# A first attention block whose turned probabilities and outputs are taken out of PSUM by ScalarE, one and two steps behind its exponentials

## The reference, cut to what matters

```python
s = jnp.einsum('bqhgd,bkhd->bhgqk', q_blk, k_blk).astype(jnp.float32) * scale
s = jnp.where(valid, s, MASK_VALUE)
m = jnp.maximum(jnp.max(s, axis=-1, keepdims=True), sink)
p = jnp.exp(s - m)
p = p / (jnp.sum(p, axis=-1, keepdims=True) + jnp.exp(sink - m))
return jnp.einsum('bhgqk,bkhd->bqhgd', p.astype(v_blk.dtype), v_blk)
```

```python
z = y @ w_glu.astype(jnp.float32) + b_glu.astype(jnp.float32)
out = z[..., :SSM_WIDTH] * jax.nn.sigmoid(z[..., SSM_WIDTH:])
```

## Time and profile before

| what | value |
|---|---|
| runs of the kernel, us | 2356.20, 2364.24, 8599.52 |
| median, us | 2364.24 |
| profiled execution, us | 2353.87, of which the span from first to last instruction 2352.0 |
| TensorE matmuls busy | 2193.4 us, 93% of the span |
| VectorE busy | 1278.7 us, 54% |
| ScalarE busy | 901.6 us, 38% |
| GpSimd busy | 91.5 us, 4% |
| granted TensorE clock, mean | 0.961 |
| first turn's eight steps | about 159.5 to 202 us |
| second turn's eight steps | about 207.2 to 251 us |

### The profile page before, as it was taken

The page is one execution under the profiler, slowest core; times in us unless marked ns, Lnnn a source line. Parts: engine busy times, 40 slices in busy tenths (PEclk is TensorE's granted clock), DMA queues, the critical chain, the costliest instruction groups (busy, mean ns, idle before and its releaser), DMA issues.

```text
span 2352.0 us, 29837 instructions
## 1 busy us (share of the span) xinstructions
PE 2193.4 (93%) x11134; PEld 1795.0 (76%) x11134; DVE 1278.7 (54%) x1993; ACT 901.6 (38%) x1299; POOL 91.5 (4%) x99
## 2 busy tenths in 40 slices
PE   7858899999998999999997899999999978999997
PEld 6735778888876888888875788888777867888886
DVE  6965454434445566655565743244568876433444
ACT  4224332322225556555642432232244424422422
POOL 1000120000040000000000000000000000000000
PEclk9979899999999999999998999999899989999998
DMA  4001213232132222222211222232112212232221
GB/s 160 29 10 37 89 54 107 77 105 105 69 110 81 81 85 69 80 72 85 76 67 39 76 101 90 91 105 90 63 63 72 71 55 72 89 99 98 89 90 54
DMA packets 32091, 185.54 MB, mean 79 GB/s; under 512 B 4736, under 2 KB 5120, under 8 KB 13312
## 3 DMA queue, kind: packets, MB, share of 16 engines
q1 hardware_dynamic: 27216, 176.17, 21.7%
q10 hardware_dynamic: 2736, 6.00, 0.7%
q0 software_dynamic: 2048, 2.17, 0.4%
HBM read 180.06 MB, written 2.10 MB: 77 GB/s over the span
## 4 chain that ended last, share of the span: by engine, by line
PE 82%; DVE 10%; DVEq 4%; ACT 2%; issue 2%; ACTq 0%; DMA 0%; POOL 0%; POOLq 0%
PE ps L517 12%; PE ps L518 12%; PE ps L519 12%; PE ps L908 5%; PE ps L910 5%; PE ps L909 5%; PE ps L950 3%; PE ps L951 3%; PE ps L952 3%; PE ps L540 2%; PE ps L579 2%; PE ps L542 2%; PE ps L541 2%; DVE f_run L2245 1%; PE ps L846 1%
## 5 line engine op out<-in xcount | busy, mean ns | idle before, releaser
L1084 ACT ACTIVATE w_hi<-raw 128x2048 fp32r<-128x2048 f32 x122 | 232.8, 1908 | 298.0 <-PE ps L519 217.0
L517 PE MATMUL ps<-x_hi,w_lo 128*128 128x512 f32 x864 | 336.9, 390 | 5.8 <-DVE w_lo L1481 3.6
L519 PE MATMUL ps<-x_hi,w_hi 128*128 128x512 f32 x864 | 336.2, 389 | 0.0
L518 PE MATMUL ps<-x_lo,w_hi 128*128 128x512 f32 x864 | 336.2, 389 | 0.0
L1481 DVE TENSOR_TENSOR w_lo<-raw,w_hi 128x2048 fp32r<-128x2048 f32 x122 | 280.0, 2295 | 83.3 <-ACT w_hi L1084 82.9
L908 PE MATMUL ps<-x_hi,w_lo 128*128 128x512 f32 x560 | 225.2, 402 | 6.3 <-DVE w_lo L2061 6.3
L910 PE MATMUL ps<-x_hi,w_hi 128*128 128x512 f32 x560 | 219.6, 392 | 0.0
L909 PE MATMUL ps<-x_lo,w_hi 128*128 128x512 f32 x560 | 218.5, 390 | 0.0
L517 PEld LDWEIGHTS ps<-x_hi,w_lo 128*128 128x128 f32 x864 | 162.2, 188 | 41.5 <-DVE w_lo L1481 4.5
L519 PEld LDWEIGHTS ps<-x_hi,w_hi 128*128 128x128 f32 x864 | 162.2, 188 | 33.8
L518 PEld LDWEIGHTS ps<-x_lo,w_hi 128*128 128x128 f32 x864 | 162.2, 188 | 33.2
(11 more groups left out here) (403 smaller groups left out, 4020.0 us busy)
## 6 DMA issues: line engine op xcount, KB each, us to landing
raw<-w_attn_in SPq DMA_DIRECT2D x32, 1024.0 KB, 4.9
raw<-w_gate_up SPq DMA_DIRECT2D x22, 1024.0 KB, 4.9
raw<-w_up_a SPq DMA_DIRECT2D x16, 1024.0 KB, 4.9
raw<-w_down_a SPq DMA_DIRECT2D x16, 1024.0 KB, 4.9
raw<-w_up_h SPq DMA_DIRECT2D x16, 1024.0 KB, 4.9
raw<-w_down_h SPq DMA_DIRECT2D x16, 1024.0 KB, 4.8
raw<-w_hgrn_in SPq DMA_DIRECT2D x8, 1024.0 KB, 4.9
raw<-w_down SPq DMA_DIRECT2D x8, 768.0 KB, 4.3
```

Of the source, the lines that this page charges most:

```text
L517: pe.matmul(o, w_lo[:, slot, a:a + P], hi[:, k, :], start=k == 0, stop=False)
L518: pe.matmul(o, w_hi[:, slot, a:a + P], lo[:, k, :], start=False, stop=False)
L519: last = pe.matmul(o, w_hi[:, slot, a:a + P], hi[:, k, :], start=False, stop=k == st.kc - 1)
L1084: act.activation(w_hi[:, slot, :], raw[:, slot, :], ACT.Copy).then_inc(whi_ready, 1)
```

## The change

The copy of the turned probabilities and the two scalings of the outputs go from VectorE to ScalarE. On ScalarE, step s now holds the exponentials of s, then `turned_out(s-1)` (the copy), then `scale_out(s-2)` (the scalings, written as a Copy with a per-row scale). Behind step 7 stand `turned_out(7)`, `scale_out(6)` and `scale_out(7)`, and then `gate(1, i)`. `gate(0, i)` stands behind `scale_out(3)`. VectorE keeps the sum and the reciprocal (`invert1`), which now wait for `p1_ready` and tell ScalarE by a new semaphore, `inv1_ready`. TensorE's list doesn't change.

```diff
--- before.py
+++ after.py
@@ -357,6 +357,7 @@
     p1t_done, p1t_ready = sem("p1t_done"), sem("p1t_ready")
     o1_done, o1_ready = sem("o1_done"), sem("o1_ready")
     o1t_done = sem("o1t_done")
+    inv1_ready = sem("inv1_ready")
     h_back = sem("h_back")
     vt2_done = sem("vt2_done")
     rot_ready = sem("rot_ready")
@@ -1172,6 +1173,20 @@
                 act.activation(tmp[:, c, :], ps[:, GLU_BANKS[2 * c + 1], :], ACT.Sigmoid,
                                bias=gains[:, ds(2 * i + GAIN_AT["b_glu"] + 4 + c, 1)]).then_inc(gate_ready, 1)
 
+            def turned_out(s, i):
+                n = BLOCKS1[s % 4][1]
+                act.wait_ge(p1t_done, 8 * i + s + 1)
+                act.activation(p1_t[:, s % 2, 0:2 * n * P], ps[:, (5, SUM)[s % 2], 0:2 * n * P], ACT.Copy).then_inc(p1t_ready, 1)
+
+            def scale_out(s, i):
+                hh, b = s // 4, BLOCKS1[s % 4][0]
+                act.wait_ge(o1_done, 8 * i + s + 1)
+                act.wait_ge(inv1_ready, 8 * i + s + 1)
+                for m in range(2):
+                    last = act.activation(o1_tok[:, b, ds(256 * i + 128 * m + 64 * hh, 64)], ps[:, 6, 64 * m:64 * m + 64],
+                                          ACT.Copy, scale=stat[:, s % 4, 12 + m:13 + m])
+                last.then_inc(o1_ready, 1)
+
             with act.Fori(0, 2) as i:
                 for s in range(8):
                     hh, (b, n) = s // 4, BLOCKS1[s % 4]
@@ -1185,8 +1200,15 @@
                         act.activation(p1[:, s % 4, 2 * P * m:2 * P * m + n * P], ps[:, 3 + s % 2, 2 * P * m:2 * P * m + n * P],
                                        ACT.Exp, bias=st_[:, 4 + m:5 + m], scale=0.125, accum_out=st_[:, 8 + m:9 + m])
                     act.activation(st_[:, 6:8], st_[:, 6:8], ACT.Exp).then_inc(p1_ready, 1)
+                    if s >= 1:
+                        turned_out(s - 1, i)
+                    if s >= 2:
+                        scale_out(s - 2, i)
                     if s == 5:
                         gate(0, i)
+                turned_out(7, i)
+                scale_out(6, i)
+                scale_out(7, i)
                 gate(1, i)
 
 
@@ -1844,35 +1866,23 @@
                     ts(st_[:, 4:6], st_[:, 2:4], -1.0, None, ALU.mult)
                     tt(st_[:, 6:8], sinks, st_[:, 2:4], ALU.subtract).then_inc(max1_ready, 1)
 
-                def scale1(s):
-                    hh, (b, n) = s // 4, BLOCKS1[s % 4]
+                def invert1(s):
                     st_ = stat[:, s % 4, :]
+                    dve.wait_ge(p1_ready, 8 * i + s + 1)
                     tt(st_[:, 10:12], st_[:, 6:8], st_[:, 8:10], ALU.add)
                     settle()
-                    dve.reciprocal(st_[:, 12:14], st_[:, 10:12])
-                    settle()
-                    dve.wait_ge(o1_done, 8 * i + s + 1)
-                    for m in range(2):
-                        last = ts(o1_tok[:, b, ds(256 * i + 128 * m + 64 * hh, 64)],
-                                  ps[:, 6, 64 * m:64 * m + 64], st_[:, 12 + m:13 + m], None, ALU.mult)
-                    last.then_inc(o1_ready, 1)
+                    dve.reciprocal(st_[:, 12:14], st_[:, 10:12]).then_inc(inv1_ready, 1)
 
                 maximum1(0)
                 maximum1(1)
                 for s in range(8):
-                    n = BLOCKS1[s % 4][1]
                     if s % 4 == 0:
                         split_lo(glu_st, s // 4, i)
                     if s == 6:
                         glu(0, i)
-                    dve.wait_ge(p1t_done, 8 * i + s + 1)
-                    dve.tensor_copy(p1_t[:, s % 2, 0:2 * n * P], ps[:, (5, SUM)[s % 2], 0:2 * n * P]) \
-                        .then_inc(p1t_ready, 1)
+                    invert1(s)
                     if s < 6:
                         maximum1(s + 2)
-                    if s:
-                        scale1(s - 1)
-                scale1(7)
                 glu(1, i)
             for c in range(4):
                 dve.wait_ge(o1t_done, c + 1)
```

## The result

The change makes the kernel slower by 0.4%: ratio 1.0040, interval 1.0025 to 1.0055, over 20 runs of each. The medians are 2356.37 us before and 2366.18 us after, so +9.8 us. The 20 runs before include the three shown ahead of the prediction; their median was high by 8 us. The profiled execution of the change took 2361.97 us (span 2360.2), that of before 2353.87 (span 2352.0): +8.1 us.

A forecast was written before the change was run, and what follows sets the result against it. TensorE's own work, 82% of the span, was taken as the bound. Two turns x 0.2 + 1.6 + 2.0 gave +4.0 us; on the shown runs 2360.2 and 2368.2, so the forecast was 2362, range 2352 to 2376.

The forecast's parts named there:

- What bounds the kernel, and what the move costs by itself: Attention loop: TensorE's own work bounds; moved pairs take about 0.50 us on ScalarE, and steps 0 to 4 cost nothing.
- Step 5, the late gate: `gate(0)` behind `scale_out(3)` delays step 6's turn 1.35 us, mostly within an existing wait: +0.2 us a turn.
- The end of a turn: `gate(1)` behind `scale_out(7)` comes into the open: +1.6 us before the second turn, +2.0 us behind the loop.
- the 3.2 to 5.5 of the working: Ends of the summed loss in us, for pairs at 0.4 or 0.7 us and shorter or longer handovers.
- The double-switch rival: Each of three table loads a turn costs twice its 1.28 us: +11.7 us in all, 2370; chance 0.05.
- the sum: Two turns x 0.2 + 1.6 + 2.0 = +4.0 us, on the profiled execution 2357.9 us.
- a rival with a chance of 0.15: Longer TensorE pauses bring one more piece of low clock: +4 and +5, so +9 us, 2367; chance 0.15.
- The prediction's own sign: From the first scores to the first `w_out` matmul, about 4 us more.
- The working's own number: The +4.0 us added to a base time; the forecast of 2362 was put between 2360.2 and 2368.2.
- the verdict of within 2%: Whole kernel: chance 0.97 of a time within 2% of before, faster 0.01, slower 0.02.
- VectorE's relief: TensorE's waits for `o1_tok` and `y` go and the tail is hidden: -3.3 us, 2355; chance 0.11.
- ScalarE's round: Steps of the loop: ScalarE's round and waits exceed TensorE's step, time over 2411; chance 0.02.

The follow-up runs named there:

- the tail on VectorE: The changed kernel with the scalings of steps 6 and 7 returned to VectorE: 2352.62 us against 2351.86 before, ratio 1.0001.
- the candidate: The change with scalings of steps 6 and 7 on VectorE, step 4's weight split later, `gate(0)` ahead of `scale_out(3)`: 2344.34 us against 2354.42 before, ratio 0.9955.
- the wait alone: The kernel before, nothing moved, with ScalarE's last gate of a turn made to wait for VectorE's last scaling: 2365.88 us against 2351.86, ratio 1.0066.
- without the switch: The changed kernel with `gate(1, i)` as a plain Copy, no Sigmoid or table load there: 2361.94 us against 2354.42 before, ratio 1.0033.
- the candidate with the late tail: The candidate with scalings of steps 6 and 7 on ScalarE again, ahead of the last gate: 2357.60 us, ratio to before 1.0017.
- filling them: Unread bfloat16 matmuls added in TensorE's pauses: in the changed kernel 2363.35 us, in the kernel before 2357.22, both against 2351.86.
- the gate one place earlier: The changed kernel with `gate(1, i)` between `turned_out(7, i)` and `scale_out(6, i)`: 2363.49 us against 2354.42 before, ratio 1.0028.
- the copies alone: The kernel before with only the eight copies a turn moved to ScalarE: 2357.00 us against 2354.42, ratio 0.9997; its profiled execution took 2377.2 us.

## Why the prediction was wrong

**What bounds the kernel, and what the move costs by itself: right.** Pairs of scalings took 0.52 us (0.50 forecast), copies 0.60. TensorE has no new wait in steps 1 to 4. All copies and twelve of sixteen scalings a turn, for the steps 0 to 5, cost nothing (ratio 1.0001 with the tail on VectorE).

**Step 5, the late gate: right.** The timeline of TensorE in step 6:

```profile
193.21 0.66 PE L737 MATMUL ps<-consts,p 128*128 128x128 f32 x4 [1.22 <-ACT stat L1202]
193.62 0.48 PE L755 MATMUL ps<-x_hi,w_lo 128*128 128x512 f32 x1
```

The turn waits 1.22 us for the exponentials, and the gated matmul follows without a wait. Counted from the first scores it starts 0.29 us later than before (34.59 against 34.30), 0.2 forecast. At the end of the turn this is gone again: the last pair ends at 42.24, before 42.28, because ScalarE starts its pair 0.1 us behind the values (200.75), VectorE did so 0.5 behind them (201.40). That isn't a trait of the engines: in the candidate VectorE's last pair starts 0.15 us behind the values.

**The end of a turn: right mechanism, sized too small.** Forecast +1.6 and +2.0, measured +2.25 twice. Two terms were short. The step from `y` to VectorE's next instruction: I took 0.14 us from a place within a step, and at the loop's branch it is 0.65 (203.46 + 0.75 to 204.86), behind the loop 0.3. The row 203.21 of the earlier trace rows has a gap of 0.67 us ahead of the rotation, and I put it down to TensorE's swap alone; the same 0.66 or 0.67 stands there in the change, where the swap had ended 0.8 us before `y` did, with the wait alone, without the switch and in both candidates. And the step from ScalarE's Sigmoid to VectorE's `y`: 0.04 was taken from no row, and it is 0.18 and 0.16 (203.28 to 203.46, 256.85 to 257.01). The two pauses, 4.5 us, still lie within the 3.2 to 5.5 of the working. Of the table load itself nothing was wrong: 1.28 us, at 201.29, 0.02 behind the scaling's end. The double-switch rival counted three loads a turn; the timeline has a fourth, ahead of the split behind `gate(1)` (203.29), and none of TensorE's waits shown above names it. The drain that the Trainium skill's page (ScalarE: Activation LUTs, What ACT_TABLE_LOAD costs) adds to a switch isn't in this trace either, so that rival falls.

**The step that failed: clock at nothing in the sum.** The sum held the pauses only, +4.0, and put a further low stretch into a rival with a chance of 0.15, at +9 us. That rival's amount is what was measured, +9.8: the mean clock over 20 runs of the change is 0.9568, over 23 to 35 runs of before 0.9597 to 0.9598, which is about 14 us more at 1.2 GHz, part of it during pauses. "Against it: the clock is already low behind both" was the wrong step. It looked at where the clock was low, not at how long it stayed there: behind the loop the low stretch went from about 15 to 25 us, and one of 7 us came in steps 4 and 5 of the second turn. The prediction's own sign says the same: about 4 us more to the first `w_out` matmul, and it was 11.8. In the change, with the wait alone and in the candidate with the late tail the loss is 5 to 9 us above the pauses. That the late gate brings it is shown, by adding the wait alone and by taking the tail away twice. The rival's reason, that longer pauses bring it, isn't: filling them was no clean test, a kernel with half the pauses (the gate one place earlier) had as low a clock, and one long run of the copies alone had the low stretch in the second turn without them. So the hit of +9 is in part luck, and what ties gate and clock stays open.

**The base.** The forecast of 2362 was hung between the profiled execution and a median of three runs of which one was far off. That median, 2364.24, was 8 us above what 20 runs give. So 2362 stood below the median shown, though the working said slower by 4. The working's own number on the true median would have been 2360.4, and 2366.2 was measured. The range held the time, and the verdict of within 2% is right, but a forecast of the direction should have been put on the same base as the number.

**The other rivals.** VectorE's relief paid nothing by itself. ScalarE's round never became the bound: the exponentials of step 7 ended at 195.04, and TensorE's turn of them started at 195.93 without a wait.

## What to carry to other kernels

When work moves onto an engine, look first at what stands behind it in that engine's list, at the last item above all: here two pairs of small scalings that wait for TensorE pushed a Sigmoid, with its table load, from under the last values into the open, while the other fourteen pieces of a turn, eight copies and six such pairs, cost nothing that could be measured. Price the gap at a loop's branch from a row at a branch. And where a kernel's runs spread with the granted clock, take the clock's mean over many runs beside the medians, since a single profile shows one throw.

A candidate that beats both kernels came out of it, 0.45% faster than before: split the slab of the next turn behind the exponentials of steps 4 to 6, and keep the last two pairs of scalings of a turn off the gate's engine.

## What the runs showed of the hardware

The loss in time was two to three times the growth of the pauses wherever the whole gate stood behind the last scaling: +9.8 us for 4.5 (the change), +14.0 for 5.0 (the same gate on the kernel before), +13.3 for 4.6 on the candidate. Low clock makes up the rest, and 35 runs of one unchanged kernel lie 21 us apart with their mean clock between 0.951 and 0.965. Small matmuls pay for it: the first thirty-two sums of 128x1 behind the loop took 4.0 us before, nearly all of it at 2.4 GHz, and 6.8 us in the change at 1.2. The second thirty-two took 6.8 us at 1.2 GHz in both kernels.

A table load takes 1.28 us and stands as it is in ScalarE's list: it starts 0.02 us behind the instruction ahead of it, and the Sigmoid 0.02 us behind the load. Between VectorE's last instruction of a turn and the first of the next lie 0.66 us, against 0.14 within a step and 0.29 behind the loop.
